# Token mixing on one core: where the second half of the input projections is computed, and how retention is staged

## The reference, cut to what matters

```python
h = rmsnorm(x, attn_norm_g[l])
proj = h @ w_in[l]                       # 1024 -> 3072: dq dk dv rq rk rv rg
dq, dk = rotate_prefix(dq, ...), rotate_prefix(dk, ...)
a = diff_attention(dq, dk, dv, lam)      # 4 heads: softmax(map 0) - lam * softmax(map 1), times dv
a = rmsnorm(a, diff_norm_g[l]) * (1.0 - lambda_init)
rq, rk = rotate_prefix(rq, ...), rotate_prefix(rk, ...) * RET_QK_DIM ** -0.5
r = retention(rq, rk, rv, decay)         # 4 heads, both directions: (q k^T * decay) v
r = silu(rg) * group_norm(r, ret_norm_g[l])
x = x + concat([a, r]) @ w_out[l]
```

## Time and profile before

| | us |
|---|---|
| median of 3 runs | 3322.12 (3318.9 to 3324.98) |
| the profiled execution's own time | 3321.03 |
| its span (first to last instruction) | 3319.3 |
| mean granted TensorE clock | 0.966 of full |
| busy: PE, DVE, ACT, POOL | 3112.4, 1748.6, 1081.7, 472.6 |
| HBM traffic over the span | 106 GB/s |

### The profile page before, as it was taken

How to read it: one execution, slowest core, us unless ns; L and a number is a source line. 1 busy time by engine, 2 the same in 40 slices (tenths; PEclk the granted TensorE clock), 3 DMA queues, 4 the chain that set the end, 5 groups by cost and what they waited for, 6 DMA issues and landing times. The chain is left out here.

```text
span 3319.3 us, 40685 instructions
## 1 busy us (share of the span) xinstructions
PE 3112.4 (94%) x14652; PEld 2461.3 (74%) x14652; DVE 1748.6 (53%) x3020; ACT 1081.7 (33%) x1536; POOL 472.6 (14%) x296
## 2 busy tenths in 40 slices
PE   8968899999999999999999999878978999999998
PEld 6622678878887888788888888658957878678886
DVE  4362439979955555444444444655444435444444
ACT  3142423224434443222223323331232325432222
POOL 0000004554442222000000000124400000000000
PEclk9985899999999999999999999989989999999999
DMA  4200223444565445333333332210012223123321
GB/s 140 79 0 11 90 76 112 135 139 179 223 242 206 170 173 201 114 121 118 116 119 126 120 120 90 86 32 10 1 38 77 95 82 127 51 76 95 95 94 70
DMA packets 105605, 352.94 MB, mean 106 GB/s; under 512 B 10241, under 2 KB 11137, under 8 KB 103970
## 3 DMA queue, kind: packets, MB, share of 16 engines
q1 hardware_dynamic: 105506, 351.65, 31.7%
HBM read 299.18 MB, written 52.43 MB: 106 GB/s over the span
## 5 line engine op out<-in xcount | busy, mean ns | idle before, releaser
L129 ACT ACTIVATE weights_hi<-weights_raw 128x1024 fp32r<-128x1024 f32 x459 | 478.2, 1052 | 776.2 <-PE psum L146 369.6
L160 PE MATMUL psum<-act_hi,weights_hi 128*128 128x512 f32 x1368 | 545.9, 399 | 32.7 <-DVE act_lo L348 15.6
L137 DVE TENSOR_TENSOR weights_lo<-weights_raw,weights_hi 128x1024 fp32r<-128x1024 f32 x399 | 502.5, 1266 | 91.4 <-ACT weights_hi L129 90.5
L160 PE MATMUL psum<-act_lo,weights_hi 128*128 128x512 f32 x1368 | 543.0, 397 | 0.0
L160 PE MATMUL psum<-act_hi,weights_lo 128*128 128x512 f32 x1368 | 542.9, 397 | 0.0
L146 PE MATMUL psum<-inner_hi,weights_hi 128*128 128x512 f32 x1280 | 506.5, 396 | 2.3 <-DVE inner_lo L1499 2.1
L146 PE MATMUL psum<-inner_hi,weights_lo 128*128 128x512 f32 x1280 | 505.6, 395 | 0.0
L146 PE MATMUL psum<-inner_lo,weights_hi 128*128 128x512 f32 x1280 | 505.6, 395 | 0.0
L160 PEld LDWEIGHTS psum<-act_hi,weights_hi 128*128 128x128 f32 x1368 | 258.5, 189 | 101.6 <-issue 35.5
L160 PEld LDWEIGHTS psum<-act_hi,weights_lo 128*128 128x128 f32 x1368 | 258.6, 189 | 62.7
L160 PEld LDWEIGHTS psum<-act_lo,weights_hi 128*128 128x128 f32 x1368 | 258.8, 189 | 62.3 <-issue 0.5
(11 more groups left out here) (351 smaller groups left out, 4437.7 us busy)
## 6 DMA issues: line engine op xcount, KB each, us to landing
weights_raw<-in_u_experts SPq DMA_DIRECT2D x256, 512.0 KB, 3.7
gates_dram<-gates_stage SPq DMA_DIRECT2D x8, 4096.0 KB, 12.1
gates_of_group<-gates_dram SPq DMA_DIRECT2D x16, 2048.0 KB, 11.0
weights_raw<-in_u_mlp SPq DMA_DIRECT2D x64, 512.0 KB, 3.6
ups_dram<-up_products SPq DMA_DIRECT2D x64, 256.0 KB, 2.2
up_group<-ups_dram SPq DMA_DIRECT2D x8, 2048.0 KB, 8.9
weights_raw<-in_u_in SPq DMA_DIRECT2D x24, 512.0 KB, 3.7
weights_raw<-in_u_merge SPq DMA_DIRECT2D x24, 512.0 KB, 3.6
```

What stands on the lines that cost most here:

```text
L129: self.nc.scalar.activation(self.hi[slot][:, :, :], self.raw[:, slot, :].rearrange("p (c n) -> p c n", c=C), ACT.Copy).then_inc(self.hi_re ...
L137: eng.tensor_tensor(self.lo[slot][:, :, :], self.raw[:, slot, :].rearrange("p (c n) -> p c n", c=C), self.hi[slot][:, :, :].bitcast(F32), ...
L160: mm = self.nc.tensor.matmul(out, w[slot][:, c, :], a[:, j, 0:tokens], start=first and n == 1, stop=last and n == 3 * len(chunks))
```

## The change

1. The first `linear` makes slabs 0 to 11 (attention's queries, keys and values) only. The operand `act_hi`, `act_lo` stays allocated, and is later reused as `mix_hi`, `mix_lo`.
2. Stages 2 and 3 become one. It transposes the four attention value heads, rotates the 8 attention slabs, and runs the 16 attention steps. PE computes the other 12 units in pieces of 2 chunks behind each value head and each rotation, and of 4 and 5 chunks in turn at the beginning of each attention step (`project`). ACT and DVE split their weights and DVE reads them out of PSUM (`split`, `read`) between the steps. The scores of step `it + 2` are now issued behind the transposes of step `it`, and have two pairs of PSUM banks instead of three. SP issues the weight loads behind the tables.
3. The next stage holds what retention needs (four rotations, four transposed value heads), retention itself by pairs of heads (8 steps; both heads' scores from the two halves of the partitions, one behind the other), and the first head norm: its squares, averages, roots and split are spread over PE, ACT and DVE in that stage. Each head's decay keeps its own buffer.
4. The attention result goes to slabs 0 to 3 of `proj`, retention's to slabs 4 to 7, instead of to a tensor of their own.

The amount of arithmetic is the same. Cut to its core (8 columns of indentation removed):

```diff
 ctx.enter_context(mix_stack)
 proj = sb("projections", [P, IN_SLABS, T], F32, mix_stack)
-act_stack = ExitStack()
-act_hi = sb("act_hi_a", [P, C, T], F32R, act_stack)
...
-linear(IN_SLABS, (act_hi, act_lo), scaled(lambda n: proj[:, n, :]), "vector", prologue=True, norm=(x, 0), before=load_start)
-act_stack.close()
+act_hi = sb("act_hi_a", [P, C, T], F32R, mix_stack)
+act_lo = sb("act_lo_a", [P, C, T], F32R, mix_stack)
+linear(RQ, (act_hi, act_lo), scaled(lambda n: proj[:, n, :]), "vector", prologue=True, norm=(x, 0), before=load_start)
...
-mix_hi = sb("mix_hi", [P, C, T], F32R, mix_stack)
-mix_lo = sb("mix_lo", [P, C, T], F32R, mix_stack)
-v_tok = sb("values_by_token", [P, 2 * HEADS, T], F32, mix_stack)
+mix_hi, mix_lo = act_hi, act_lo
...
+tables = sb("rope_tables_sb", [P, 4, T], F32, mix_stack)
+swaps = sb("rope_swaps", [P, 2, P], F32, mix_stack)
...
-rotary = [(n, 0) for n in range(DQ, DV)] + [(n, 1) for n in range(RQ, RV)]
-values = list(range(DV, DV + HEADS)) + list(range(RV, RV + HEADS))
...
+rest_read = sig("later_projection_read")
...
+REST = IN_SLABS - RQ
+TURNS, ROPES = HEADS, len(diff_rotary)
+BEFORE = TURNS + ROPES
+chunks_in = [2] * BEFORE + [(REST * C - 2 * BEFORE) * (it + 1) // steps - (REST * C - 2 * BEFORE) * it // steps for it in range(steps)]
+chunks_before = [sum(chunks_in[:n]) for n in range(BEFORE + steps + 1)]
...
@@ -670,52 +691,146 @@
...
+        w.load_stage(sp, REST)
...
+        def project(n):
+            for q in range(chunks_before[n], chunks_before[n + 1]):
+                u, c = divmod(q, C)
+                if c == 0 and u >= 2:
+                    pe.wait_ge(rest_read.sem, u - 1)
+                mm = w.multiply_chunk(pe, 0, u, 0, psum[:, 6 + u % 2, :], (act_hi, act_lo), c)
+                if c == C - 1:
+                    mm.then_inc(w.unit_done.sem, 1)
...
+        for j in range(TURNS):
             if j >= 2:
...
+            project(j)
...
+        for j, n in enumerate(diff_rotary):
...
+            project(TURNS + j)
+        pe.wait_ge(rope_done.sem, ROPES)
+        pe.wait_ge(v_copied.sem, TURNS)
+        scores(0)
+        scores(1)
+        for it in range(steps):
+            h, q = divmod(it, TT)
+            project(BEFORE + it)
+            pe.wait_ge(combined.sem, it + 1)
+            if it >= 1:
+                pe.wait_ge(turned_read.sem, it)
+            for kt in range(TT):
+                mm = nc.tensor.transpose(psum[:, 4, kt * P:(kt + 1) * P], amap[:, it % 2, kt * P:(kt + 1) * P], ident[:])
+            mm.then_inc(turned.sem, 1)
+            if it + 2 < steps:
+                scores(it + 2)
+            if q == TT - 1:
+                pe.wait_ge(turned_read.sem, it + 1)
+                if h >= 1:
+                    pe.wait_ge(mixed_read.sem, h)
+                for kt in range(TT):
+                    mm = nc.tensor.matmul(psum[:, 5, :], v_tok[:, h, kt * P:(kt + 1) * P],
+                                          amap_t[:, h % 2, kt, :], start=kt == 0, stop=kt == TT - 1)
+                mm.then_inc(mixed.sem, 1)
...
+        for j in range(TURNS):
+            split(j)
             act.wait_ge(v_turned.sem, j + 1)
...
+        for j in range(ROPES):
+            split(TURNS + j)
...
+        exps(0)
+        for it in range(steps):
+            h, q = divmod(it, TT)
+            split(BEFORE + it)
+            if it + 1 < steps:
+                exps(it + 1)
+            act.wait_ge(turned.sem, it + 1)
+            if h >= 2:
+                act.wait_ge(mixed.sem, h - 1)
+            nc.scalar.activation(amap_t[:, h % 2, :, q * P:(q + 1) * P], psum[:, 4, :].rearrange("p (k q) -> p k q", k=TT),
+                                 ACT.Copy).then_inc(turned_read.sem, 1)
+            if q == TT - 1:
+                act.wait_ge(mixed.sem, h + 1)
+                nc.scalar.activation(diff_out[:, h, :], psum[:, 5, :], ACT.Copy).then_inc(mixed_read.sem, 1)
...
+        def read(n):
+            for u in units_ended(n):
+                dve.wait_ge(w.unit_done.sem, w.done(u))
+                nc.vector.tensor_tensor(proj[:, RQ + u, :], psum[:, 6 + u % 2, :], rstd[:, :], ALU.mult).then_inc(rest_read.sem, 1)
...
+        for j, n in enumerate(diff_rotary):
+            if j:
+                read(TURNS + j - 1)
+            else:
+                for turn in range(TURNS):
+                    read(turn)
             dve.wait_ge(rope_swapped.sem, j + 1)
...
+            nc.vector.tensor_tensor(by_sin[:, j % 2, :], psum[:, j % 2, :], tables[:, 1, :], ALU.mult).then_inc(rope_sin.sem, 1)
...
             nc.vector.tensor_tensor(proj[:, n, :], by_cos[:, j % 2, :], by_sin[:, j % 2, :], ALU.add).then_inc(rope_done.sem, 1)
+            split(TURNS + j)
...
         maxima(0)
         maxima(1)
+        dve.wait_ge(lam_step.sem, 4)
...
                 dve.wait_ge(turned.sem, it - 1)
             nc.vector.scalar_tensor_tensor(amap[:, it % 2, :], probs[:, it % 2, 1, :], stats[:, it, 7:8], probs[:, it % 2, 0, :],
                                            ALU.mult, ALU.add).then_inc(combined.sem, 1)
+            read(BEFORE + it - 1)
+            split(BEFORE + it)
             if it + 2 < steps:
                 maxima(it + 2)
-
-head_norm(heads_out, average128[:], eps_ap[:, 0:1], center=False, split_to=(gain_d, mix_hi, mix_lo))
+        read(BEFORE + steps - 1)
+weights.u0 += REST
...
+    by_cos = sb("rope_by_cos", [P, 4, T], F32, local)
+    by_sin = sb("rope_by_sin", [P, 4, T], F32, local)
     dist = sb("ret_distances", [P, 2, SPAN], F32, local)
-    args = sb("ret_decay_log", [P, 2, SPAN], F32, local)
-    decay = sb("ret_decay", [P, 2, SPAN], F32, local)
-    weighed = sb("ret_scores", [P, 4, T], F32, local)
+    decay = sb("ret_decay", [P, HEADS, SPAN], F32, local)
+    weighed = proj[:, DV:DV + HEADS, :]
+    squares, diff_rstd = by_cos, by_sin
+    pair_steps = HEADS // 2 * TT
...
-            if it >= 4:
-                pe.wait_ge(ret_decayed.sem, it - 3)
...
+            pair, kt = divmod(it, TT)
+            if it >= 2:
+                pe.wait_ge(ret_decayed.sem, 2 * (it - 1))
...
+                nc.tensor.matmul(psum[:, 2 * (it % 2) + g, :], proj[rows, RK + pair, kt * P:(kt + 1) * P], proj[rows, RQ + pair, :],
+                                 start=True, stop=True).then_inc(ret_scored.sem, 1)
+        for j, n in enumerate(ret_rotary):
+            nc.tensor.matmul(psum[:, j, :], swaps[:, 1, :], proj[:, n, :], start=True, stop=True).then_inc(rope_swapped.sem, 1)
+        for j in range(HEADS):
+            for tile in range(TT):
+                mm = nc.tensor.transpose(psum[:, 4 + j, tile * P:(tile + 1) * P], proj[:, RV + j, tile * P:(tile + 1) * P], ident[:])
+            mm.then_inc(v_turned.sem, 1)
+        pe.wait_ge(rope_done.sem, ROPES + 4)
...
+        for it in range(pair_steps):
+            pair, kt = divmod(it, TT)
+            for g in range(2):
+                h = 2 * pair + g
+                pe.wait_ge(ret_decayed.sem, 2 * it + g + 1)
+                nc.tensor.matmul(psum[:, 4 + h, :], v_tok[:, h, kt * P:(kt + 1) * P], weighed[:, 2 * (it % 2) + g, :],
+                                 start=kt == 0, stop=kt == TT - 1).then_inc(ret_mixed.sem, 1)
+            if it + 2 < pair_steps:
...
-                             start=kt == 0, stop=kt == TT - 1).then_inc(ret_mixed.sem, 1)
+            if it == pair_steps - 2:
+                for j in range(HEADS // 2):
+                    pe.wait_ge(gn_square.sem, gn_square.at(j + 1))
+                    nc.tensor.matmul(psum[:, j, :], average128[:], squares[:, j, :], start=True, stop=True).then_inc(gn_var.sem, 1)
+        pe.wait_ge(ret_decayed.sem, 2 * pair_steps)
+        for j in range(HEADS // 2, HEADS):
+            pe.wait_ge(gn_square.sem, gn_square.at(j + 1))
+            nc.tensor.matmul(psum[:, j, :], average128[:], squares[:, j, :], start=True, stop=True).then_inc(gn_var.sem, 1)
...
+        for j in range(HEADS):
+            act.wait_ge(v_turned.sem, TURNS + j + 1)
+            nc.scalar.activation(v_tok[:, j, :], psum[:, 4 + j, :], ACT.Copy).then_inc(v_copied.sem, 1)
...
+            nc.scalar.activation(decay[:, h, :], decay[:, h, :], ACT.Exp).then_inc(decay_ready.sem, 1)
+        act.wait_ge(rope_done.sem, ROPES + 4)
+        for h in range(HEADS):
+            nc.scalar.activation(squares[:, h, :], diff_out[:, h, :], ACT.Square).then_inc(gn_square.sem, 1)
+        for j in range(HEADS):
+            act.wait_ge(gn_var.sem, gn_var.at(j + 1))
+            nc.scalar.activation(diff_rstd[:, j, :], psum[:, j, :], ACT.Ln, bias=eps_ap[:, 0:1], scale=1.0).then_inc(gn_log.sem, 1)
+        for h in range(HEADS):
+            act.wait_ge(ret_mixed.sem, 2 * TT * (h // 2) + 2 * (TT - 1) + h % 2 + 1)
+            nc.scalar.activation(ret_out[:, h, :], psum[:, 4 + h, :], ACT.Copy)
+        for j in range(HEADS):
+            act.wait_ge(gn_log.sem, gn_log.at(j + 1))
+            nc.scalar.activation(diff_rstd[:, j, :], diff_rstd[:, j, :], ACT.Exp, scale=-0.5).then_inc(gn_rstd.sem, 1)
```

(38 more changed lines are left out.)

184 lines of the change are left out of this document (63 added, 121 removed).

## The result

The changed kernel takes **3240.2 us** (median of 4 runs, 3237.24 to 3242.4) against 3321.47 of the kernel before in the same rounds (4 runs, 3318.9 to 3324.98): a ratio of 0.9754, with a 95% interval of 0.9737 to 0.9771. Forecast were 3245, within 3238 to 3270. Run again later in the study, the same kernel gave 3236.14 (5 runs, 3234.16 to 3240.07; ratio 0.9746 [0.9733, 0.976]), which is 1.9 us under the lower end of the range. One execution of a later kernel (the one with both edits) took 3873.84 us at a granted clock of 0.743, in a slow state of the chip, and is left out of that kernel's ratio.

A forecast was written before the change was run, and what follows sets the result against it. Bound by projections, then rotation and attention chains over DVE, and retention on PE at 1.2 GHz. Second head norm at 208.0 + 36 + 14.3 = 258.3 instead of 334.96, -76.7, gives 3244.3; plus 0.7, 3245 us; range 3238 to 3270.

The forecast's parts named there:

- Part 1: Dense projection loop: 12 of 24 units leave, 67.2 us, so the rotation stage starts at 82.7.
- Part 2: Four value heads and eight rotations, two chunks each: 7.9 and 18.0 plus about 1.9; scores start 27.8 us in.
- Part 3: Attention with 4 or 5 chunks a step at 2.4 GHz: 97.5 us, ending at 208.0.
- 16 handovers of 0.1 us: Attention: 0.1 us for each of 16 steps' handovers, added beside the steps' 79.5 and the values' 14.5.
- the terms 0.58, 3.63 and 1.8: Attention's end: four transposes 0.58, values at a head's end 3.63, last copy and barrier 1.8 us.
- Part 4: Retention by head pairs: first value matmul after 11.7 us, last ends after 36, then 14.3 to the second head norm.
- a low start: Retention: 1.5 us added for a low clock at its start, before 2.4 GHz after a step or two.
- (a): Rival: retention stays at 1.2 GHz, 5.7 us a step, +22: 3267 us; chance 0.13.
- (b): Rival: attention bound by its scores-to-map path, with DVE's read and split in it, +14: 3259 us; chance 0.07.
- (c): Rival: nothing overlaps in attention, transposes queue behind chunks, 10.0 us a step: 3342 us; chance 0.03.
- (d): Rival: no gain, moved units fill time PE then lacks, attention's clock at 1.2 GHz: 3321 us; chance 0.01.

The follow-up runs named there:

- the one with both edits: Changed kernel plus four unread matmuls in PE's waits at retention's start, gate activations and two heads' copies ahead of the logarithms: 3232.91 us; again 3234.08.
- the kernel with nothing spread: Changed kernel with all 24 units back in the dense loop and no chunks in rotations or attention steps: 3308.25 us, ratio 0.9953 to the kernel before.
- the kernel with pairs between: Changed kernel with each pair of retention scores computed twice, once behind each single value matmul: 3244.61 us (1 run).
- the alternating kernel: Changed kernel with retention's pairs undone, one head's 64-row score and one 128-row value matmul in turn: 3266.07 us, ratio 0.9828 to the kernel before.
- the kernel with late chunks: Changed kernel with each attention step's chunks moved behind the transposes, ahead of the scores: 3290.39 us (1 run).

## Why the prediction was right, and where its terms were off

The forecast put the second head norm at 258.3; it is at 253.42. The 4.9 us are the sum of the four parts below (0.9, 2.1 and 2.4 too long, 0.5 too short). They are not the whole story of 3245: that number stands for a profiled execution of 3244.3, and the profiled one took 3237.24, 7.1 less, of which the other 2.2 lie in the unchanged stretch behind, where they are chance. That the median came out 4.8 under the forecast, next to 4.9, is luck, and so is the side of the range's lower end on which it fell: 3240.2 lies in 3238 to 3270, the repeat's 3236.14 doesn't. What held are the mechanism and the steps; the sum was some 5 us too long.

- **Part 1** said 82.7 for the start of the rotation stage; it is 81.8. A unit takes 5.60 us as before, and the first projection matmul starts at 10.25 us where it started at 10.23. What differs lies right behind: the chunk matmuls go from one every 0.43 us to one every 0.23 at 13.8 us in this execution and at 15.9 in the one before. In the repeat that is at 16.1 and the stage starts at 83.0, so this term is what one execution differs from another by.
- **Part 2** said 27.8 us; it took 25.7. Rotations are at 2.25 each, exactly. The four value heads took 7.4 for 7.9 (81.86 to 89.22). The term of 1.9 us, "for two places at which DVE's split makes PE late and for the last sum, which nothing covers", was mis-sized: it is 0.3 (107.55, less 89.22 and eight times 2.25). The last sum is covered, by the two chunks behind the eighth rotation (PE waits 0.19 at 107.55), and VectorE, busy for 16.8 of 25.7 us, catches up after a split before PE runs short.
- **Part 3** said 97.5 us; it took 95.1. Steps of 5.15 and 4.80 were measured at 5.19 and 4.77. The mis-sized term is the 16 handovers of 0.1 us, 1.6: they had no place beside those steps, for they lie inside them. A head's values with the step behind them took 7.94 (129.23 to 137.17) for 8.08, three times, and the first step 7.6 for 7.9. The end of the stage held: 5.93 us from the last transposes to the next stage (196.68 to 202.61), where the terms 0.58, 3.63 and 1.8 give 6.0. The clock of 1.00 came as assumed; that it depends on the chunks, and is not simply granted to this stage, only the kernel with nothing spread showed.
- **Part 4** said 11.7 us to the first value matmul (11.6), 36 to the end of the last (36.5) and 14.3 from there (14.3). The step of 2.97 us is exact. The 1.5 us for a low start was right for this execution and chance as such: the same kernel had no low start when it ran again, and took 49.2 instead of 50.8. The change of rows costs 0.2 us each time at full clock, so 0.4 a step and not 0.2 (the other 0.2 lie inside the pair's 1.06): in the kernel with pairs between, a single value matmul behind a change takes 1.06 where one without takes 0.85. The Trainium skill ("TensorEngine Tiling (Array Packing)", Key Properties) says that changing the tiling mode drains TensorE; the traces agree, with these 0.2 us at full clock, and 0.3 for each change in the alternating kernel, whose pitch is 2.00 for 1.71 at half clock.

**Rivals.** (a), retention at 1.2 GHz, was the one with substance. The alternating kernel is the nearest case, but not the same: (a) kept the pairs and had 5.7 us a step, the singles in turn take 8.0 for the same work. That it gave 3266 where (a) said 3267 is chance, for (a) was added to a sum that was some 5 us too long. What kept the changed kernel out of it is not, as I had argued, that only work on all rows raises the clock; the clock rose as well in a stage with half of its matmuls on 64 rows, where its full ones came two in a row. (b) did not happen: behind the first step VectorE waits for PE. (c), nothing overlapping, is the side on which the kernel with late chunks lies, though it stays faster than the kernel before: 3290 for the 3342 of (c), since exponentials and maxima are a step ahead in it too. (d) fell with 1.00 in attention.

Not tried: another division of the units than these, and an order of the tail in which ScalarE's last splits stand behind the gates. What in TensorE's order makes the clock rise is told only by the four orders seen here.

## What to carry over

When a stage is bound by a chain over other engines, look for dense work with no dependence on it and place it on the waiting engine directly ahead of the wait, behind what feeds the chain: against the bare loop in the same order it cost nothing until it was as long as the chain (3.05 us), and one place later it hid nothing at all. Price the new order without the work as well: here the bare loop alone was 31.8 us slower than the one it replaced. Count the clock with it, since with the waits filled the stage's own matmuls ran at 2.4 GHz, and read the granted clock of every dense stage too: matmuls on 64 rows in turn with full ones ran 26 to 30 us longer than the same ones in pairs.

## What was not expected of the hardware

- A TensorE busy in 50.00 of 50.00 us stayed at 0.50 of its clock when single 64-row matmuls and single 128-row ones alternated, and did not in two orders that differ from it only slightly (above), though all three had started retention with a fall of the clock.
- The clock can fall while TensorE is busy: in the kernel with both scores from one half of the rows it did so within a run of four scores, behind a wait of 1.93 us, and was back at 1.00 only from 220; in the changed kernel it fell from 215 to 216, behind the start of the first value matmul, and was back by 219.
- The same program had 0.50 at the start of retention in one profile and 1.00 in another, behind the same waits of 1.93 and 2.27 us. The Trainium skill ("TensorE: Matmul & The Clock Gate", Part 4) says that transposes don't count as busy, on which I had leaned for the low start; the same 16 transposes stand ahead in both, so the runs neither bear it out nor deny it.
